# A streaming-encoder trunk on one core: in the S5 stage SyncE stores the input of tile c+2 ahead of loading that of tile c+1

## The reference, cut to what matters

```python
def s5_mixer(hn, w_in, lam_re, lam_im, log_step, b_re, b_im, c_re, c_im, d_skip, w_out):
    u = (hn @ w_in).astype(jnp.float32)
    ug = u.reshape(bsz, seq, S5_GROUPS, S5_GROUP_CH).astype(jnp.complex64)
    ...
    bu = jnp.einsum('bsgc,gpc->bsgp', ug, b_bar)
    _, states = lax.associative_scan(combine, (a, bu), axis=1)
    y = jnp.einsum('bsgp,gcp->bsgc', states, c).real.reshape(bsz, seq, D_MODEL)
    y = y + d_skip.astype(jnp.float32) * u
    h = jax.nn.gelu(y).astype(hn.dtype)
    vg = h @ w_out
    return vg[..., :D_MODEL] * jax.nn.sigmoid(vg[..., D_MODEL:])
```

## Time and profile before

| | us |
|---|---|
| runs | 3266.08, 3276.89, 3277.32 |
| median of the runs | 3276.89 |
| span of the profiled execution | 3272.8 |
| TensorE matmul busy | 3167.1 (97%) |
| VectorE busy | 2267.4 (69%) |
| ScalarE busy | 1691.8 (52%) |
| GpSimd busy | 821.7 (25%) |
| granted TensorE clock, mean over the span | 0.988 |

### The profile page before, as it was taken

How to read it: one execution, slowest core, us unless ns; L and a number is a source line. 1 busy time by engine, 2 the same in 40 slices (tenths; PEclk the granted TensorE clock), 3 DMA queues, 4 the chain that set the end, 5 groups by cost and what they waited for, 6 DMA issues and landing times.

```text
span 3272.8 us, 62859 instructions
## 1 busy us (share of the span) xinstructions
PE 3167.1 (97%) x19574; PEld 2770.4 (85%) x19574; DVE 2267.4 (69%) x4218; ACT 1691.8 (52%) x3583; POOL 821.7 (25%) x1372
## 2 busy tenths in 40 slices
PE   5999999999989999999999998999999999999998
PEld 4989898989878888888888887888888888888887
DVE  5777777777756588667886767875667645775566
ACT  5565656565644455444555555324555444454444
POOL 1000000000010189888888830661000000000000
PEclk8999999999999999999999999999999999999999
DMA  6444444444447777777777876886666676666754
GB/s 163 120 123 110 129 107 128 112 121 119 116 132 182 202 200 208 210 201 207 200 203 202 209 194 179 239 243 171 181 188 186 179 188 185 180 183 177 182 152 141
DMA packets 1047697, 560.62 MB, mean 171 GB/s; under 512 B 47664, under 2 KB 1035472, under 8 KB 1047104
## 3 DMA queue, kind: packets, MB, share of 16 engines
q1 hardware_dynamic: 980608, 495.38, 56.7%
q10 hardware_dynamic: 58160, 37.63, 4.0%
q0 software_dynamic: 8848, 26.59, 2.6%
HBM read 530.40 MB, written 29.13 MB: 171 GB/s over the span
## 4 chain that ended last, share of the span: by engine, by line
PE 79%; DVE 9%; DMA 4%; issue 4%; ACT 3%; SPq 1%; ACTq 1%; DVEq 0%; POOL 0%; POOLq 0%
PE bank L293 44%; PE bank L294 22%; PE bank L637 5%; DVE w_lo L281 4%; DMA u_scratch<-u 3%; ACT w_hi L275 1%; DVE tiles L1929 1%; DVE normed L1941 1%; PE bank L635 1%; DVE tiles L308 1%; SPq L477 1%; PE bank L698 1%; PE bank L711 0%; PE bank L600 0%; PE bank L751 0%
## 5 line engine op out<-in xcount | busy, mean ns | idle before, releaser
L293 PE MATMUL bank<-act,w_hi 128*128 128x512 f32 x4352 | 1586.3, 406 | 19.6 <-DVE act L330 8.1
L281 DVE TENSOR_TENSOR w_lo<-raw,w_hi 128x512 fp32r<-128x512 f32 x1856 | 1308.2, 755 | 190.6 <-ACT w_hi L275 177.7
L294 PE MATMUL bank<-act,w_lo 128*128 128x256 f32 x4352 | 1217.5, 280 | 0.0
L293 PE MATMUL bank<-mid,w_hi 128*128 128x512 f32 x3072 | 1096.0, 401 | 21.8 <-DVE mid L1943 13.9
L275 ACT ACTIVATE w_hi<-raw 128x512 fp32r<-128x512 f32 x1856 | 1040.2, 621 | 87.1 <-PE bank L294 64.5
L293 PEld LDWEIGHTS bank<-act,w_hi 128*128 128x128 f32 x4352 | 819.8, 188 | 213.5 <-DVE w_lo L281 13.4
L294 PE MATMUL bank<-mid,w_lo 128*128 128x256 f32 x3072 | 865.8, 282 | 0.0
L294 PEld LDWEIGHTS bank<-act,w_lo 128*128 128x128 f32 x4352 | 823.0, 189 | 5.0 <-issue 4.1
L293 PEld LDWEIGHTS bank<-mid,w_hi 128*128 128x128 f32 x3072 | 583.0, 190 | 165.8 <-DVE mid L1943 15.1
L294 PEld LDWEIGHTS bank<-mid,w_lo 128*128 128x128 f32 x3072 | 586.3, 191 | 0.0
L303 ACT ACTIVATE tiles<-bank 128x256 f32<-128x256 f32 x384 | 146.3, 381 | 597.4 <-PE bank L294 593.2
(11 more groups left out here) (325 smaller groups left out, 2945.4 us busy)
## 6 DMA issues: line engine op xcount, KB each, us to landing
raw<-in_mlp_w_up_dram SPq DMA_DIRECT2D x128, 1024.0 KB, 6.4
raw<-in_mlp_w_down_dram SPq DMA_DIRECT2D x128, 1024.0 KB, 6.1
raw<-in_gdn_w_in_dram SPq DMA_DIRECT2D x96, 1024.0 KB, 5.9
raw<-in_gdn_w_out_dram SPq DMA_DIRECT2D x32, 1024.0 KB, 6.5
raw<-in_ple_w_gate_dram SPq DMA_DIRECT2D x32, 1024.0 KB, 6.1
raw<-in_s_w_out_dram SPq DMA_DIRECT2D x28, 1024.0 KB, 6.8
raw<-in_s_w_in_dram ACTq DMA_DIRECT2D x10, 1024.0 KB, 12.6
c_scratch<-c_pow ACTq DMA_DIRECT2D x32, 256.0 KB, 4.4
```

The source lines that it names most:

```text
L281: eng.tensor_tensor(w_lo[par][:, c], raw[slot][:, c], w_hi[par][:, c].bitcast(F32), ALU.subtract).then_inc(S("lo_ready"), 1)
L293: eng.matmul(a[:, :], w_hi[par][:, w], rhs[:, k0 + kt, :], start=(k0 + kt == 0), stop=False)
L294: mm = eng.matmul(a[:, 0:NT], w_lo[par][:, w], rhs[:, k0 + kt, 0:NT], start=False, stop=(k0 + kt == kend - 1))
```

## The change

SyncE's round c issues the store of tile c+2, as before, and then the loads of tile c+1 in place of those of tile c+2. The stores of the two slots of `u` count on two semaphores, u_saved0 and u_saved1, and VectorE and the loads wait on the one of their slot. SyncE's rounds are all written out. The first two tiles are stored and loaded ahead, as before; round 0 has no load, round 14 only a load (of tile 15), round 15 nothing.

```diff
             def store_u(ct, j):
 
                 sp.wait_ge(S("u_ready"), ct + 1)
-                sp.dma_start(one_of(u_dram, ct), u[:, j % 2, :, :].rearrange("p t c -> p (t c)")).then_inc(S("u_saved"), 16)
-
-            def load_uf(ct, j):
+                sp.dma_start(one_of(u_dram, ct), u[:, j % 2, :, :].rearrange("p t c -> p (t c)")).then_inc(S(f"u_saved{j % 2}"), 16)
+
+            def load_uf(ct, i, j):
 
                 if not isinstance(ct, int) or ct >= 4:
                     sp.wait_ge(S("y_done"), ct - 3)
-                sp.wait_ge(S("u_saved"), ct * 16 + 16)
+                sp.wait_ge(S(f"u_saved{j % 2}"), i * 32 + 16 * (j // 2 + 1))
...
                 ct = i * 4 + j
                 if ahead(i, j, 2):
                     store_u(ct + 2, j)
-                    load_uf(ct + 2, j + 2)
+                if ahead(i, j, -1) and ahead(i, j, 1):
+                    load_uf(ct + 1, (ct + 1) // 4, (ct + 1) % 4)
...
                         store_u(ct, ct)
-                        load_uf(ct, ct)
-                    s5_rounds(sp, s5_tile)
+                        load_uf(ct, 0, ct)
+                    for ct in range(KT):
+                        s5_tile(ct // 4, ct % 4)
...
-            def input_ready(ct, tau, par):
+            def input_ready(ct, tau, par, stored):
 
                 sum_halves(ve, tau, par, summed[:, par, :])
                 ve.wait_ge(S("acc_freed"), tau + 1)
-                if not isinstance(ct, int) or ct >= 2:
-                    ve.wait_ge(S("u_saved"), ct * 16 - 16)
+                if stored is not None:
+                    ve.wait_ge(S(f"u_saved{par}"), stored)
...
-                    input_ready(ct + 2, ct + (t0 + 2), j % 2)
+                    input_ready(ct + 2, ct + (t0 + 2), j % 2, i * 32 + 16 * (j // 2 + 1))
```

More of the change, by code:

```diff
@@ L2068, in _ @@
                         if c < 3:
-                            input_ready(c - 1, t0 + c - 1, c - 1)
+                            input_ready(c - 1, t0 + c - 1, c - 1, None)
                     s5_rounds(ve, s5_tile)
```

## The result

The kernel after takes 3289.21 us (median of 20 runs, 3275.62 to 3302.55) against 3275.82 us (20 runs, 3264.72 to 3293.38): ratio 1.0038, 95% interval 1.0027 to 1.0049. It is slower, by some 12 us (the interval is 9 to 16 us); forecast were 3279 us and a range that ended at 3287.

What follows compares the result with a forecast made beforehand. It took the kernel as bound by TensorE, paced in the S5 stage by SyncE's queue standing for each store. Early tiles +1.3, tile 13 +1.6, tile 14 +2.4, taken as +2: 3276.9 + 2 = 3279 us, range 3265 to 3287.

Steps and rivals of the forecast that it cites:

- SyncE's queue that stands for each store: S5 stage: SyncE's loads wait for the store just issued, 11.90 us a tile, which sets TensorE's rate.
- +1.9 us: Issue of the loads of tile c+1, counted from ScalarE's copy of input c+2; the old order issued at +0.5 to +1.9.
- S(c+1) = S(c-1) + 11.0 + L: Start of a tile's first TensorE matmuls (S), two tiles on: 11.0 us to ScalarE's copy, then L; 11.95 a tile.
- L: Time from ScalarE's copy of input c+2 to TensorE's start of tile c+1, set by the loads' landing; taken as 12.9 us.
- The edits costed at nothing: New semaphores, unrolled SyncE loop, VectorE's slot wait and the y_done wait: no cost, covered by SyncE's idle time.
- one 11.95, against 12.01 before: TensorE's time for one steady tile of the S5 stage, new against old order: 0.06 us less.
- Between 10.4 and 12.9 I take 11.5: Landing in the early tiles, in us after ScalarE's copy, under lighter traffic; tile 6 then starts 1.3 us later than before.
- I take 12.9, because the batch has the same content and the same place in the same burst: Landing of a steady tile's batch after ScalarE's copy, in us, as the mean of eight old batches, tiles 7 to 14.
- The end of the stage: Tile 14 starts 2.4 us later and GpSimd's last loads hang on it; stage +2.4 us, taken as +2.
- C(15): The moment when ScalarE copies the half accumulator of input 15; tile 14's start was taken as 12.9 us later.
- The base: Time of the kernel before: 3276.89 us, median of the three shown, with 4.1 us around the 3272.8 us span.
- Rival C: Loads queue behind the whole 128 KB store: L = 15.0, tiles of 13.0 us, +12 us, 3289 us; chance 0.13.

Runs made afterwards that it cites:

- e1: The kernel after with SyncE's old order back (round c: store c+2, then loads c+2), semaphores and written-out rounds kept: ratio 1.0007 to the kernel before.
- r9: The kernel after, unchanged, run once more beside the others: ratio 1.0035 to the kernel before.
- e5: Against the kernel after: loads of c+2 in round c again, stores of tiles 3 to 15 issued by GpSimd: ratio 0.9964 to the kernel before.
- e11: e5 with waits of some 2.2 us added to TensorE in tiles 3, 5, 9 and 12: ratio 1.0012 to the kernel before.
- e7: The kernel after with rounds 0 to 3 in the old order and the new one from round 5 on: ratio 1.0034 to the kernel before.
- e12: e5 with SyncE storing tile 3 too, so that GpSimd stores from tile 4 on: ratio 0.9978 to the kernel before.
- e6: The kernel before with TensorE's state_inputs moved behind the first quarter of multiply, so `uf` is needed 2.8 us later: ratio 1.0005.

## Why the prediction was wrong

**Right.** The old kernel's bound, SyncE's queue that stands for each store. That the new order issues at +1.9 us where the old one had drifted to +0.5 to +1.9, so that a wait for `uf` takes the place of the wait for the store; S(c+1) = S(c-1) + 11.0 + L gives 12.15 us a tile with the measured L, and the trace has (2215.11 - 2130.29) / 7 = 12.12. The edits costed at nothing were nothing that the runs can tell (e1, at most 0.2%).

**Wrong.** The step that failed is the sum's: it priced the new waits at their own length and let the early tiles land early.

1. *The clock had no term.* The sum has "one 11.95, against 12.01 before", and the waits of the early tiles were counted with their own length. Each long wait was followed by a stretch at half clock, which cost 3.3 us in tile 3 (14.12 - 10.82) and 6.4 us in tile 5 (17.26 - 10.82). The rows of before could have told: S(14) = 2207.13 has first matmuls of 2.51 us instead of 1.89 behind a wait of 1.45. In the stage the clock is 8.6 of the 17.7 us; by the other trace of each order (r9 less e1) it is 13.7 of 19.9.
2. *"Between 10.4 and 12.9 I take 11.5"*, the landing in the early tiles. It was 13.7 us at tile 3 (2086.06 less the copy at 2072.32) and 12.7 at tile 5, much as later. The 10.4 came from a store alone in its batch. The sum also let the new kernel wait from tile 4 on only, though its own rule gives S(3) as the copy of input 4 plus L, 10.4 us behind that copy before: every us of L above that is a wait at tile 3. From S(2) to S(6) the new kernel takes 58.5 us, the old one 45.1, forecast 46.4. These tiles hold 13.4 of the stage's 17.45 us in this trace, 9.7 of them the half clock of point 1 (3.3 and 6.4); in r9 they hold 6.0 us over before. So the size of this point is not settled.
3. *"I take 12.9, because the batch has the same content and the same place in the same burst"*: 13.3. From S(6) to S(13) that is 84.8 against 83.4 us, forecast 83.65. In r9 it is 90.9, with half clock in tiles 9 and 11.
4. *The end of the stage.* S(14) follows C(15) by 14.6 us where 12.9 were taken. Tile 13 has little work of its own, so TensorE waits 6.0 us ahead of tile 14. But e1, in the old order, waits 7.04 us there too, so this is not shown to be the new order's.
5. *The base.* 4.1 us were put around the span; 1.6 lie there (3285.64 and 3284.0 in the profiled run after). The profiled run before was thus none of the three shown, and the sum does not suffer, as it starts from the median; that moved by 1.1 us, to 3275.82.

Rival C gave 3289, which is what was measured, but by L = 15.0 and tiles of 13.0; with L at 13.3 it did not come about. Its side was right, its mechanism was not what happened. That it met the number is luck. It had 0.13 and deserved more: the costs that the sum left out (clock, early tiles) had the same sign. The range ended at "half of C", 3287, and the chance within 0.5% (0.92) was well placed.

## What to carry to other kernels

Where transfers come in bursts once a round, a small load costs what is in flight when it leaves: here 3 us at the end of a burst, 9 at its start. Tie it to the event that ends a burst (its own store's landing) and not to the one that begins the next; if a queue is blocked by waits for stores, move the stores, not the loads. And price a new wait of TensorE above its length: first its idle time, then the half clock that may follow. Here that came to about twice the length between before and after and between e5 and e11; over all traces the clock loss goes from 0.4 of the idle time (e7, e12) to 1.6 (e6).

## What the runs showed of the hardware that was not expected

Waits of 1.0 to 4.0 us of TensorE were followed by 3.4 to 13.7 us at clock 0.50, or by none: 1.87 us at tile 5 of after was followed by 13.7 us, 1.94 us at tile 12 by none; 2.19 us at tile 3 of e11 by 6.9, 2.19 us at tile 9 by none; 1.60 us at tile 11 of r9 by 13.7; 0.97 us at tile 5 of e1 by 3.4. A wait's effect on the clock is thus not fixed by its length. That this spreads the runs is not shown: the 20 runs of after lie 27 us apart, those of before 29.
